# Experts of a diffusion block: the up projection in three 256-column passes for each k

## The reference

```python
# T = 2048 latent tokens, D = 1024, E = 16 experts, D_EXPERT = 1024, cap = 2 * 2048 / 16 = 256
aff = softmax(h @ w_router)                          # (T, E)
top_aff, top_idx = top_k(aff.T, cap)                 # each expert chooses 256 tokens
xe  = h[top_idx]                                     # (E, 256, D)
hid = silu(xe @ w_gate) * (xe @ w_up)                # (E, 256, 1024)
ye  = (hid @ w_down) * top_aff                       # (E, 256, D)
out = zeros.at[top_idx].add(ye)
```

## Time and profile before

| | us |
|---|---|
| median of 3 runs (lowest, highest) | 4299.33 (4295.75, 4299.92) |
| the profiled execution's own time | 4294.17 |
| its span | 4292.6 |
| TensorE matmuls busy | 3979.8 (93%) |
| VectorE busy | 2381.5 (55%) |
| ScalarE busy | 1526.0 (36%) |
| GpSimd busy | 761.8 (18%) |

### The profile page before, as it was taken

How to read it: one execution, slowest core, us unless ns; L and a number is a source line. 1 busy time by engine, 2 the same in 40 slices (tenths; PEclk the granted TensorE clock), 3 DMA queues, 4 the chain that set the end, 5 groups by cost and what they waited for, 6 DMA issues and landing times. The chain is left out here.

```text
span 4292.6 us, 57758 instructions
## 1 busy us (share of the span) xinstructions
PE 3979.8 (93%) x20052; PEld 3059.7 (71%) x20052; DVE 2381.5 (55%) x3126; ACT 1526.0 (36%) x2467; POOL 761.8 (18%) x691
## 2 busy tenths in 40 slices
PE   8999999999979999998899999899049999999998
PEld 3444446456759999998678778788048888888886
DVE  5555410356646566664443535344876767777675
ACT  5333311225632222222342424222034444444443
POOL 3877100011113333332000000000000010101000
PEclk9999999999989999999899999999579999999999
DMA  7234241011131222221435434243056676667673
GB/s 301 89 109 116 72 116 34 16 59 37 26 134 66 83 73 73 74 87 69 155 102 173 158 104 154 84 155 137 10 183 214 214 219 211 214 210 214 204 219 94
DMA packets 234599, 542.96 MB, mean 126 GB/s; under 512 B 35163, under 2 KB 95867, under 8 KB 231803
## 3 DMA queue, kind: packets, MB, share of 16 engines
q1 hardware_dynamic: 202380, 426.69, 30.6%
q0 software_dynamic: 32112, 114.84, 9.0%
HBM read 439.95 MB, written 99.55 MB: 126 GB/s over the span
## 5 line engine op out<-in xcount | busy, mean ns | idle before, releaser
L2668 DVE TENSOR_TENSOR sb_we_low<-sb_we,sb_we_high 128x1024 fp32r<-128x1024 f32 x384 | 466.9, 1222 | 132.0 <-ACT sb_we_high L2620 131.8
L2620 ACT ACTIVATE sb_we_high<-sb_we 128x1024 fp32r<-128x1024 f32 x384 | 399.5, 1048 | 284.0 <-PE ey L2595 147.8
L303 PE MATMUL p_ps<-sb_hT,sb_ring 128*128 128x512 f32 (+1 forms) x960 | 378.2, 551 | 1.8 <-ACT sb_raw L446 1.8
L2105 DVE TENSOR_TENSOR sb_wm_low<-sb_wm,sb_wm_high 128x1024 fp32r<-128x1024 f32 x127 | 155.3, 1223 | 394.4 <-ACT sb_wm_high L2018 394.4
L2577 PE MATMUL eg<-sb_xe_parts,sb_we_high 128*128 128x512 f32 x1024 | 370.9, 395 | 1.6 <-DVE sb_xe_parts L2663 1.6
L2577 PE MATMUL eu<-sb_xe_parts,sb_we_high 128*128 128x512 f32 x1024 | 370.9, 394 | 0.0
L1960 PE MATMUL pg<-sb_hb_high,sb_wm_high 128*128 128x512 f32 x768 | 303.5, 395 | 16.1 <-DVE sb_wm_low L2105 10.8
L303 PEld LDWEIGHTS p_ps<-sb_hT,sb_ring 128*128 128x128 f32 x960 | 183.1, 192 | 188.7 <-issue 180.9
L1961 PE MATMUL pg<-sb_hb_low,sb_wm_high 128*128 128x512 f32 x768 | 300.7, 391 | 0.0
L1962 PE MATMUL pg<-sb_hb_high,sb_wm_low 128*128 128x512 f32 x768 | 300.4, 391 | 0.0
L2576 PE MATMUL eu<-sb_xe_parts,sb_we_low 128*128 128x256 f32 x896 | 251.9, 281 | 0.0
(11 more groups left out here) (408 smaller groups left out, 8523.2 us busy)
## 6 DMA issues: line engine op xcount, KB each, us to landing
sb_we<-in_w_ex SPq DMA_DIRECT2D x384, 512.0 KB, 4.4
sb_wm<-in_w_gates SPq DMA_DIRECT2D x96, 512.0 KB, 3.7
sb_wrow<-in_w_mod_row POOLq DMA_DIRECT2D x64, 256.0 KB, 3.5
sb_wm<-in_w_br SPq DMA_DIRECT2D x32, 512.0 KB, 4.5
sb_ring<-in_w_ch POOLq DMA_DIRECT2D x19, 512.0 KB, 3.6
sb_lq<-q_d SPq DMA_DIRECT2D x36, 256.0 KB, 2.6
sb_lk<-k_d SPq DMA_DIRECT2D x36, 256.0 KB, 2.9
sb_lkt<-kt_d SPq DMA_DIRECT2D x36, 256.0 KB, 3.6
```

The lines of the kernel that those rows point to most:

```text
L303: last = nc.tensor.matmul(ps[:, b % BANKS, 0:wd], w[:, kind, k], g.hT[:, k, t0:t0 + wd], start=(k == 0), stop=(k == KD - 1))
L2105: v.tensor_tensor(wl[n], w[n], wh[n], ALU.subtract).then_inc(s.wl, 1)
L2620: nc.scalar.activation(wh[:, n % CUT], w[:, n % RAW], ACT.Copy).then_inc(s.wh, 1)
L2668: v.tensor_tensor(wl[:, n % CUT], w[:, n % RAW], wh[:, n % CUT], ALU.subtract).then_inc(s.wl, 1)
```

## The change

The up tile's joined pass of 512 columns is replaced by two passes of 256 columns, high weights by low tokens and high weights by high tokens, both into the first half of the bank. With the low pass that makes three passes into the same 256 columns. The sum of the halves is then made in PSUM, the TENSOR_REDUCE of up and the tensor `su` are gone, and the product reads the up bank's first half directly. The semaphore `usum` is gone: TensorE waits for `hid`, which the product raises, before it fills an up bank again, and `hid` starts at 2 in its place, so ScalarE's wait for it is 2 higher. The gate tile is as before.

```diff
-        sg, su = (sbuf(nc, c, n, [P, 2, CAP]) for n in ("sge", "sue"))
+        sg = sbuf(nc, c, "sge", [P, 2, CAP])
...
-                        for n, bank, free in ((2 * f, pg[f % 2], s.gsum), (2 * f + 1, pu[f % 2], s.usum)):
+                        for n, bank, free in ((2 * f, pg[f % 2], s.gsum), (2 * f + 1, pu[f % 2], s.hid)):
                             pe.wait_ge(s.wl, NW * e + n + 1)
                             pe.wait_ge(free, NF * e + f + 1)
                             for k in range(KD):
                                 high, low = (x[:, n % CUT, k * P:(k + 1) * P] for x in (wh, wl))
                                 both = xe_parts[:, u, k].rearrange("p a t -> p (a t)")
+                                if bank is pu[f % 2]:
+                                    nc.tensor.matmul(bank[:, 0:CAP], low, xh[:, u, k], start=(k == 0), stop=False)
+                                    nc.tensor.matmul(bank[:, 0:CAP], high, xl[:, u, k], start=False, stop=False)
+                                    last = nc.tensor.matmul(bank[:, 0:CAP], high, xh[:, u, k], start=False, stop=(k == KD - 1))
+                                    continue
                                 if k > 0:
                                     nc.tensor.matmul(bank[:, 0:CAP], low, xh[:, u, k], start=False, stop=False)
                                 last = nc.tensor.matmul(bank[:], high, both, start=(k == 0), stop=(k == KD - 1))
...
-                        act.wait_ge(s.hid, NF * e + f + 1)
+                        act.wait_ge(s.hid, NF * e + f + 1 + 2)
                         nc.scalar.activation(hh[:, f], hid[:, f % 2], ACT.Copy).then_inc(s.hh, 1)
...
                 dve.sem_inc(s.gsum, 2)
-                dve.sem_inc(s.usum, 2)
+                dve.sem_inc(s.hid, 2)
...
                         dve.wait_ge(s.used, NW * e + 2 * f + 2)
-                        v.tensor_reduce(su[:, f % 2], pu[f % 2][:].rearrange("p (a t) -> p t a", a=2), AX_X, ALU.add).then_inc(s.usum, 1)
-                        dve.wait_ge(s.usum, NF * e + f + 1 + 2)
                         dve.wait_ge(s.sig, NF * e + f + 1)
                         if not isinstance(i, int) or e > 0 or f > 1:
                             dve.wait_ge(s.hh, NF * e + f - 1)
-                        v.tensor_tensor(hid[:, f % 2], sg[:, f % 2], su[:, f % 2], ALU.mult).then_inc(s.hid, 1)
+                        v.tensor_tensor(hid[:, f % 2], sg[:, f % 2], pu[f % 2][:, 0:CAP], ALU.mult).then_inc(s.hid, 1)
```

More of the change, by code:

```diff
@@ L2500, in experts @@
         py = [[psum(nc, c, f"ey{a}{n}") for n in range(2)] for a in range(HALF)]
-        s = sems(nc, c, "ex", "cst pick ga0 ga1 tr xh xl used wh wl gsum usum sig hid hh hl yb sc0 sc1 held " + " ".join(f"w{n}" for n in range(RAW)))
+        s = sems(nc, c, "ex", "cst pick ga0 ga1 tr xh xl used wh wl gsum sig hid hh hl yb sc0 sc1 held " + " ".join(f"w{n}" for n in range(RAW)))
         s_w = list(s[-RAW:])
```

## The result

The changed kernel is slower by 0.18%: a median of 4306.32 us (4302.48 to 4308.29, 15 runs) against 4298.61 us (4294.0 to 4301.1, 15 runs), a ratio of 1.0018 with a 95% interval of [1.0011, 1.0025]. The forecast of 4298 us, a shade faster than before, was wrong. The time is inside the stated range, and the loss is inside the 0.2% that was called "same". But it is clear of the noise, and its sign is that of rival B.

What follows compares the result with a forecast made beforehand. The prediction took TensorE's stream of passes as the bound. Its only nonzero term, -1.3 us, on the profiled 4294.17 us made 4292.9; the runs' median stands 5.2 us higher, giving 4298 us, with an 8-in-10 range of 4285 to 4313.

Steps and rivals of the forecast that it cites:

- rival B: TensorE: each fp32r matmul pays some 13 ns over its columns whatever its width; +10 us, 4309 us; chance 0.22.
- Part 1: Up tile's 512-column pass becomes two of 256 on TensorE: 1024 more matmuls, 0.3488 against 0.350 us per k, -1.3 us.
- Part 3: VectorE loses the reduction of up, 88.6 us of busy time, worth nothing while TensorE sets the pace.
- Part 4: VectorE's product reads up from PSUM: taken as 424 ns, between 340 and 680 ns, hidden behind TensorE.
- Part 5: The product frees the up bank in place of the reduction; TensorE's wait for it costs nothing.
- Part 6: Weight transfers, released by VectorE's low parts, move forward by up to 0.7 us inside a tile; worth nothing.
- A: TensorE: a pass costs in proportion to its columns, 0.1133 us for 256; -10 us, 4289 us; chance with anything below 0.27.
- C: PSUM accumulation: passes into the same 256 columns wait for the adder; +41 us, 4340 us; chance with all costing more 0.03.

Runs made afterwards that it cites:

- experiment 3: Kernel before the change with up's joined pass split in two for k = 1 to 7 in all up tiles, VectorE's reduction kept: 4307.79 us, ratio 1.0021.
- experiment 4: Kernel before the change with up's joined pass split for k = 1 to 7 only in up tiles f = 4 to 7, reduction kept: 4299.74 us, ratio 1.0001.
- experiment 7: Kernel before the change, no pass added, all eight joined passes before the eight narrow ones in gate and up tiles: 4285.27 us, ratio 0.9967.
- experiment 9: Changed kernel with TensorE's loop written out and the gate tile's eight joined passes put before its narrow ones: 4290.51 us against 4298.68 us before the change.
- experiment 10: Changed kernel, loop written out, gate tile with six joined passes first and those of the last two k split: 4288.28 us against 4298.68 us before the change.
- experiment 11: Kernel before the change, no pass added, joined passes before narrow ones in groups of six and two in gate and up tiles: 4285.96 us, ratio 0.9972.
- experiment 12: Kernel of experiment 10 with seven joined passes in place of six in the gate tile after the transposes: 4288.46 us against 4296.68 us before the change.

## Why the prediction was wrong

**Part 1 of the prediction failed, in its size and its sign.** The sum rested on s = 0.11625 us for a narrow pass among its own kind, the mean of four pairs. In the changed kernel s is 0.1177. Three of them are 0.353 against 0.350, and the term is +3.3 us where I had -1.3. The pairs could not tell it: their mean mixed two paces, 0.113 + 0.113 in up tiles and 0.120 + 0.117 in gate tiles, that don't occur mixed within a long run. Finer rows would not have helped, as the true mean of the four pairs is 0.116 as well. A 0.0014 us error in s, times 3072 passes, is 4.5 us. That turns the sign; the rest of the loss is in the next two steps.

**The gate tiles' pace was taken as fixed.** It depends on where the tile before leaves the cycle. In the changed kernel that is +1.3 us, in experiment 3 it was up to 0.039 us a tile.

**One part was missing: the loop's code.** I counted 1024 more matmuls and loads on TensorE, and not that they make each turn of its loop 256 instructions longer. That passed a limit between 1690 and 1802 recorded instructions, and cost 2 to 3 us.

**Parts 3 to 6 held.** VectorE's 88.6 us bought nothing, the product costs 0.422 us from PSUM (0.424 taken), no pass of TensorE waited for it, and the weight transfers moved nothing. The 0.5 us at the end of the last expert has no cause shown.

**Two readings were wrong, and nothing rested on them.** The experts' matmuls are 79% of the chain's last 93 us by the earlier trace rows, not nine tenths. And the merge's 36 passes don't go into the same bank: the timeline between the two rows shows six of them into another tile (pbr), at the same 0.227.

**The rivals.** B had the sign and was nearest in size (+10 us), by a mechanism that is only half right: in the slow pace a pass pays 0.1177 - 0.1067 = 0.011 us over its columns, but in the fast one 0.0066, with the same instructions. A's pace of 0.1133 exists: it stood already in the pairs of the up tiles before, and whole runs have it in experiments 4, 7 and 9 to 12. The changed kernel never reached it. C is out by experiment 10, where passes into the same columns take 0.1133.

What stays open is what the cycle is. The runs show its places, and that a run of narrow passes keeps its pace for 36 passes (12 of a gate tile and 24 of up). They don't show which part of TensorE or of its weight loads makes it, or why the down passes settle at 0.233 and the merge's at 0.2267.

## What to carry to other kernels

Where TensorE's stream of passes is the bound, the order of passes of different widths is worth trying before their number: joined ones together, then narrow ones, gave 0.3% of the whole kernel for a change of three lines. Read the pace of a pass from long runs with their first and last start, in tiles before and after the place in question, and not from a few neighbours. And when instructions are added to a loop, compare the instruction queue's packets before and after.

## What the runs showed of the hardware

- The same 256-column fp32r passes run at 0.1133 or at 0.1177 us for whole tiles, at a granted clock of 1.00. The joined ones of gate and up tiles go 0.226, 0.229, 0.232 in turn when they stand together. The narrow ones stood at 0.1133 behind a 0.229 and a 0.232, and never otherwise (519 stretches, against 1081 at 0.1177). The formula of the Trainium skill ("TensorE: Matmul & The Clock Gate", "Back-to-back issue gap") gives one time for each width, 0.109 and 0.216 us. No fp32r run here reached either.
- A loop of TensorE of 1690 recorded instructions moved no instruction packets while it turned. Those of 1802 and 1834 moved nine of 16 KB at each turn, and stalled there at most turns, by up to 0.75 us. Straight code with more packets did not stall between experts.
